# TensorE's program of eight expert jobs: one loop over all of them, or seven written out and a loop for the rest

## The reference

```python
def moe_swiglu(xt, w_router, b_router, w_gu, w_dn):
    logits = (xt @ w_router).astype(jnp.float32) + b_router.astype(jnp.float32)
    top_v, top_e = lax.top_k(logits, TOP_K)
    gates = jax.nn.softmax(top_v, axis=-1)
    ...
    def expert_block(args):
        xblk, e = args
        g, u = jnp.split(xblk @ w_gu[e], 2, axis=-1)
        return (jax.nn.silu(g) * u) @ w_dn[e]
    yb = lax.map(expert_block, (xb, block_e)).reshape(n_rows, xt.shape[1])
    ...
```

## Time and profile before

| What | Before |
|---|---|
| Median of 3 runs | 2393.02 us (2390.64 to 2393.62) |
| Profiled execution | 2392.59 us |
| Its span, first to last instruction | 2390.8 us |
| Instructions in the profile | 55761 |
| TensorE busy | 2274.5 us, 95% |
| VectorE, ScalarE busy | 752.7 us, 572.0 us |
| First matmul of the first job, last of the eighth | 1397.17 us, 2363.14 us |
| Mean granted TensorE clock | 0.981 of full |

### The profile page before, as it was taken

How to read it: one execution, slowest core, us unless ns; L and a number is a source line. 1 busy time by engine, 2 the same in 40 slices (tenths; PEclk the granted TensorE clock), 3 DMA queues, 4 the chain that set the end, 5 groups by cost and what they waited for, 6 DMA issues and landing times.

```text
span 2390.8 us, 55761 instructions
## 1 busy us (share of the span) xinstructions
PE 2274.5 (95%) x24654; PEld 1644.5 (69%) x24654; DVE 752.7 (31%) x1513; ACT 572.0 (24%) x1094; POOL 48.5 (2%) x63
## 2 busy tenths in 40 slices
PE   7999999999999999989999999899999999999996
PEld 4777877777777887768989875555555555555554
DVE  4465345445532233477377610000101010101011
ACT  4245334323322222245355410000000000000001
POOL 0000010000200000000010000000000000000000
PEclk8999999999999999999999999999999999999998
DMA  6323232324843343212234869999999999999991
GB/s 248 116 107 141 82 130 97 133 106 159 284 176 118 127 176 131 97 65 96 105 137 146 315 265 393 361 376 356 385 365 379 362 379 362 378 358 386 361 377 63
DMA packets 86755, 549.92 MB, mean 230 GB/s; under 512 B 10336, under 2 KB 13920, under 8 KB 26496
## 3 DMA queue, kind: packets, MB, share of 16 engines
q1 hardware_dynamic: 76176, 521.91, 57.3%
q0 software_dynamic: 4176, 14.81, 1.9%
q10 hardware_dynamic: 6176, 9.70, 1.3%
HBM read 529.47 MB, written 16.91 MB: 229 GB/s over the span
## 4 chain that ended last, share of the span: by engine, by line
PE 44%; issue 43%; DVE 8%; ACT 2%; DMA 1%; POOL 0%; ACTq 0%; POOLq 0%; SPq 0%; DVEq 0%
PE pp L1363 9%; PE pp L1365 8%; PE pp L1364 8%; PE S L1363 2%; DVE wsp L926 2%; PE S L1364 2%; PE S L1365 2%; PE T L1365 2%; PE T L1363 2%; PE T L1364 2%; PE pp L1398 1%; PE T L1494 1%; ACT wsp L622 1%; PE O L1481 1%; PE S L1461 1%
## 5 line engine op out<-in xcount | busy, mean ns | idle before, releaser
L1691 PE MATMUL S<-slabs,M 128*32 128x256 f32 x7168 | 480.7, 387 | 37.3 <-issue 37.3
L1691 PEld LDWEIGHTS S<-slabs,M 128*32 128x32 f32 x7168 | 229.1, 112 | 201.2 <-issue 59.3
L926 DVE TENSOR_TENSOR wsp<-raw,wsp 128x1024 fp32r<-128x1024 f32 (+3 forms) x248 | 264.0, 1086 | 323.8 <-ACT wsp L622 322.6
L1363 PE MATMUL pp<-hx,wsp 128*128 128x512 f32 (+1 forms) x800 | 285.0, 356 | 19.8 <-DVE M L1137 4.7
L1333 DVE TENSOR_TENSOR M<-M,S 128x256 f32<-128x256 f32 x56 | 23.6, 421 | 865.2 <-ACT M L892 865.2
L1691 PE MATMUL O<-slabs,M 128*32 128x256 f32 x5376 | 294.9, 379 | 0.0
L1691 PE MATMUL T<-slabs,M 128*32 128x256 f32 x3584 | 279.8, 385 | 0.0
L1365 PE MATMUL pp<-hx,wsp 128*128 128x512 f32 (+1 forms) x800 | 277.4, 347 | 0.0
L1364 PE MATMUL pp<-hx,wsp 128*128 128x512 f32 (+1 forms) x800 | 277.4, 347 | 0.0
L1691 PEld LDWEIGHTS O<-slabs,M 128*32 128x32 f32 x5376 | 173.1, 110 | 114.9 <-issue 1.3
L622 ACT ACTIVATE wsp<-raw 128x1024 fp32r<-128x1024 f32 (+3 forms) x248 | 224.2, 935 | 28.8 <-PE pp L1365 19.9
(11 more groups left out here) (215 smaller groups left out, 2342.5 us busy)
## 6 DMA issues: line engine op xcount, KB each, us to landing
slabs<-in_w_moe SPq DMA_DIRECT2D x336, 1024.0 KB, 7.2
raw<-in_w_main SPq DMA_DIRECT2D x84, 1024.0 KB, 4.9
M<-in_w_main SPq DMA_DIRECT2D x40, 1024.0 KB, 5.0
raw<-in_w_br SPq DMA_DIRECT2D x24, 512.0 KB, 3.6
xm<-in_w_main SPq DMA_DIRECT2D x8, 1024.0 KB, 5.0
raw<-in_w_dn SPq DMA_DIRECT2D x8, 768.0 KB, 4.2
moe_rows<-M POOLq DMA_DIRECT2D x14, 384.0 KB, 9.6
raw<-in_w_dn SPq DMA_DIRECT2D x8, 640.0 KB, 3.9
```

The source lines that it names most:

```text
L926: dve.tensor_tensor(wsp[:, slot, 1, 0:w], raw[:, rslot, half * w:half * w + w], wsp[:, slot, 0, 0:w], ALU.subtract).then_inc(lo_done, 1)
L1363: mm(dst, w_hi, x_hi, start=first, stop=False)
L1691: ins = mm(banks[g // 2][32 * c:32 * c + 32, 256 * (g % 2):256 * (g % 2) + 256], x(k, g), slab_e[i % RAW_E][:, 1024 * k + 256 * c:1024 * k ...
```

## The change

The body of PE's job loop becomes a function `job(j)`. It is called seven times with the Python numbers 0 to 6, which writes seven copies into the instruction stream, and then once inside a loop from 7 to `n_jobs`. In the seven copies every wait compares with a constant. A new constant `MIN_JOBS` = 8 stands for the least number of jobs; VectorE writes the larger of it and the computed number, with a `tensor_scalar` in place of a `tensor_copy`. The loops of SP, ACT and DVE stay.

```diff
+MIN_JOBS = NE
...
-            own.link(dve.tensor_copy(jobs[0:1, N_LIST:N_LIST + 1], end[0:1, 7:8]))
+            own.link(dve.tensor_scalar(jobs[0:1, N_LIST:N_LIST + 1], end[0:1, 7:8], float(MIN_JOBS), None, ALU.max))
...
-            n_jobs = pe.value_load(jobs[0:1, N_LIST:N_LIST + 1], min_val=1, max_val=MAX_JOBS)
+            n_jobs = pe.value_load(jobs[0:1, N_LIST:N_LIST + 1], min_val=MIN_JOBS, max_val=MAX_JOBS)
...
-            with pe.Fori(0, n_jobs) as j:
+            def job(j):
+
                 def products(i, x, banks, first, last):
 
                     pe.wait_ge(e_raw[i % RAW_E], j * (16 * JOB_SLABS // RAW_E) + 16 * (i // RAW_E + 1))
...
                         ins.then_inc(e_gath, 1)
+
+            for j in range(MIN_JOBS - 1):
+                job(j)
+            with pe.Fori(MIN_JOBS - 1, n_jobs) as j:
+                job(j)
```

More of the change, by code:

```diff
@@ L532, in _ @@
             sp.wait_ge(routed, 1)
-            n_jobs = sp.value_load(jobs[0:1, N_LIST:N_LIST + 1], min_val=1, max_val=MAX_JOBS)
+            n_jobs = sp.value_load(jobs[0:1, N_LIST:N_LIST + 1], min_val=MIN_JOBS, max_val=MAX_JOBS)
             def rows_of(j):
@@ L878, in _ @@
             act.wait_ge(routed, 1)
-            n_jobs = act.value_load(jobs[0:1, N_LIST:N_LIST + 1], min_val=1, max_val=MAX_JOBS)
+            n_jobs = act.value_load(jobs[0:1, N_LIST:N_LIST + 1], min_val=MIN_JOBS, max_val=MAX_JOBS)
             def take_rows(j):
@@ L1317, in _ @@
             dve.wait_ge(routed, 1)
-            n_jobs = dve.value_load(jobs[0:1, N_LIST:N_LIST + 1], min_val=1, max_val=MAX_JOBS)
+            n_jobs = dve.value_load(jobs[0:1, N_LIST:N_LIST + 1], min_val=MIN_JOBS, max_val=MAX_JOBS)
             for n in range(2):
```

## The result

| | Before | After |
|---|---|---|
| Median of the runs | 2392.91 us (4 runs, 2390.64 to 2393.62) | 2339.39 us (4 runs, 2338.46 to 2340.74) |
| Profiled execution | 2392.59 us | 2339.31 us |
| Its span | 2390.8 us | 2337.5 us |
| First product to last product | 1397.17 to 2363.14: 965.97 us | 1396.44 to 2308.96: 912.52 us |
| TensorE busy | 2274.5 us, 95% | 2258.6 us, 97% |

The ratio of the two is 0.9778, with a 95% interval of 0.9761 to 0.9795: 53.5 us less. The whole of it, 53.45 us, lies in the expert stage; the stages ahead of it end 0.7 us earlier and the tail behind it is 0.9 us longer, since its 32 matmuls took 6.25 us in place of 5.31 (in a tail with a mean granted clock of 0.61 of full in place of 0.69).

What follows compares the result with a forecast made beforehand. TensorE was taken to bound the kernel, with pauses at its job loop's jumps back. Removing 37.3 + 14.65 = 51.95 us, less 0.02, turned 2392.59 into 2340.7; median forecast 2341, own range 2337 to 2345, range given up to 2351.

Steps and rivals of the forecast that it cites:

- Seven jumps go: Between TensorE's jobs in the expert stage: the seven long jumps back, and their pauses, vanish, taking away 37.3 us.
- The slow restart goes: TensorE's work behind each pause: the half clock there goes with the pauses, 14.65 us or 2.1 per job.
- Loop entry: TensorE's loop entry, moved to between jobs 6 and 7: costs between 0 and 7.4 us, taken as 0.
- Rival A: Between jobs 6 and 7: entering the loop acts as a jump to unfetched code, 7.4 us more, 2348; chance 0.07.
- Waits with constants: TensorE's transpositions: each loses two sequencer instructions; gain between 0 and 20 us, taken as 0.
- Rival F: TensorE's weight loads: the 0.4 us holes ahead of transpositions go too, 20 us less, 2321; chance 0.02.
- The new wait at a job's head: A job's first matmul now waits for `e_xg`, made early; boundary residue 0 to 2.9 us for seven, taken as 0.
- ACT is late next: At a job's border: ACT is ready 6.1 us into the next job, its silu due at 10.6; cover 4 us and more.
- The slabs: Expert stage DMAs: 345.91 MB must move in 914 us, 378 GB/s against 358; cost 0.
- Rival B: Expert stage: without pauses the DMAs' lead is eaten up and slabs become the bound, up to 9 us, 2350; chance 0.04.
- rival C: TensorE in the expert stage: the clock falls even without any pause, so the 14.65 us stay, 2356; chance 0.03.
- rival E: Written-out jobs: each of 124 code pieces waits 0.6 us, 74 us less the 52 saved, 2415; chance 0.03.

## Why the prediction was right, point by point

- **What bounds the stage.** That TensorE's jumps did, and not the slabs, is shown by the result, by the 28 us that four jumps cost, and by the rest without a jump that gives the time back to within 0.5 us of the stage.
- **Seven jumps go, 37.3 us.** They went, all of them. That the branch waits for the fetch is shown by the hinted loops and by the pieces that land 1.4 to 1.7 us before each dear branch ends.
- **The slow restart goes, 14.65 us.** It went. It was an inference from one job that had none. In the trace of before the granted clock is 0.50 for 6.8 us from 1514.2 us, behind an idle time that began at 1511.42, and TensorE is busy for 3.60 of them; behind each of the other six jumps it is 0.50 for 3.4 or 6.8 us, and 1.00 from 1381.1 to 1514.2, with job 0 in it. TensorE's busy time in the seven stretches is 29.9 us together; if work at half the clock takes twice as long, 15.0 of them were lost, beside the forecast's 14.65. That the cause is the idle time, the runs show: the rest of 5.3 us, with the half clock behind it and without a jump, and the rest of 1.1 us, without the half clock.
- **Loop entry, 0.** Right: 912.52 us with the loop and without it. Rival A is dead.
- **Waits with constants, 0.** Right: the rows of 23.1 and 3.3 us are unchanged. Rival F is dead. The reading of the hole as `128*32` matmuls that run out fits the starts: at all 64 places, before and after, the first weight load of the transposition begins 0.41 us behind the end of the last one before it, and 0.07 us ahead of the modelled end of the last `128*32` matmul.
- **The new wait at a job's head, 0 to 2.9 us, taken as 0.** The size was off. It is below nothing: where a job follows without a pause, its first matmuls overlap the last ones by 0.18 us. Eight jobs at 114.25 us are 914.0, the stage is 912.52. Seven overlaps make 1.3 of these 1.5 us, and jobs that are 0.03 shorter the rest. They are what separates the forecast of 2340.7 from the 2339.31 of the profiled execution, since the 0.7 us ahead of the stage and the 0.9 behind it nearly cancel. I had taken zero for the least that a border can cost and should have read how matmuls follow each other inside a job.
- **ACT is late next, cover 4 us and more.** It never came to bear. At the border at 1966.66 us its table load ended at 1970.23 + 1.28 = 1971.5, and it then waited for TensorE:

```profile
1970.23 1.28 ACT L893 ACT_TABLE_LOAD   x1 [2.37 <-issue]
1977.27 0.38 ACT L893 ACTIVATE M<-S 128x256 f32<-128x256 f32 x1 [5.76 <-PE T L1693]
```

- **The slabs, 378 GB/s, 0.** 379 GB/s and no wait, though 395 to 396 in jobs 1 to 6. Rival B named the right thing that moves, the landing (7.1 to 8.2 us), but the ring's lead of 24 us swallowed it.
- **VectorE's instruction, 0.02 us.** It took 0.142 us, the same as the copy: nothing in place of 0.02.
- **The clock, rival C.** The granted clock is 1.00 from 1380.1 to 2311.9 us, 931.8 us without a fall, in a stretch that has TensorE at work for 927.52:

```profile
1380.10:2311.90 931.80, 927.52 (x16492) 555.09 (x16490) 67.73 (x204) 56.14 (x156) 3.93 (x4) 1.00 0.95 373
```

- **Straight code fetched too late, rival E.** No idle time in any job.

The prediction told the dear jump from the cheap ones by the body that it jumps over, and that held. Up to a body of 1536 instructions the traces have 0.21 to 0.22 us for a taken branch on TensorE and 76 to 88 ns for the exit; over a body of 2016, or a job's 4130, the fetch is paid: 3.5 us quiet and 6.0 to 6.1 loaded for the one, 6.05 to 7.03 for the other.

## What to carry to other kernels

Read the sequencer's branch rows before unrolling: here a median of 6.2 us beside an exit of 83 ns was a fetch, and TensorE paid twice for each, 5.3 us by the idle time and 2.1 by the clock that fell behind it. Writing the loop out removed both at no cost in fetch, since the long body was fetched in every iteration anyway (142 pieces with the loop, 128 without); only the engine that bounds the stage needed it, and ACT and SP kept their loops. A rest of 1.1 us cost itself and 0.2 us of lost overlap, one of 5.3 us cost 2.2 more.

## What the runs showed of the hardware that I had not expected

- The fetch behind a jump on TensorE grows with the DMA traffic: 3.3 to 3.9 us on quiet queues, 5.9 to 6.2 at 421 GB/s, 6.1 to 7.0 in the job loop at some 370.
- A branch prefetch hint took such a jump from 6.1 to 0.38 us in one loop, loaded, and only to 4.2 in the job loop. The place of the loop in its blocks of 256 instructions decides whether the branch waits (head at slot 0, 3.67 to 4.75 us) or the code 48 instructions behind it (slot 208, 3.24 to 3.82 us): a branch ends 1.4 to 1.7 us after the piece that was on its way has landed.
- Neighbouring matmuls on four column groups overlap across a job's border by 0.18 us, so that a pause costs that much beside its length.
